# Input projection of a hybrid decoder trunk: twelve of thirteen products in the two-bank, 512-column form

## What is computed

```python
z = x @ w_in[l]                      # 256 x 1024 times 1024 x 6400
z_s5, z_lx, z_ly, z_rw, z_gate = jnp.split(z, IN_SPLITS, axis=-1)
y_s5  = s5_branch(z_s5, ...)         # diagonal complex state space, scan, gelu(...)
y_lru = rglru_branch(z_lx, z_ly, ..) # conv, gates, scan; y = h * gelu(z_ly)
y_rw  = rwkv7_branch(z_rw, ...)      # token shift, low-rank gates, delta-rule state
gates = sigmoid(z_gate)
merged = gates[0]*y_s5 + gates[1]*y_lru + gates[2]*y_rw
```

## Time and profile before

| What | Value |
|---|---|
| Time, median of three runs | 1608.58 us (1608.37 to 1609.64) |
| Profiled execution: span from first to last instruction | 1606.9 us |
| Profiled execution: its own whole time | not given; the span lies 1.7 us under the median |
| PE busy | 1578.1 us, 98% of the span |
| DVE, ACT, POOL busy | 1248.4, 795.6, 223.1 us |
| Mean granted TensorE clock | 0.997 |

### The profile page before, as it was taken

How to read it: one execution, slowest core, us unless ns; L and a number is a source line. 1 busy time by engine, 2 the same in 40 slices (tenths; PEclk the granted TensorE clock), 3 DMA queues, 4 the chain that set the end, 5 groups by cost and what they waited for, 6 DMA issues and landing times. The chain is left out here.

```text
span 1606.9 us, 31358 instructions
## 1 busy us (share of the span) xinstructions
PE 1578.1 (98%) x13277; PEld 1419.2 (88%) x13277; DVE 1248.4 (78%) x1624; ACT 795.6 (50%) x1018; POOL 223.1 (14%) x163
## 2 busy tenths in 40 slices
PE   9999999999999999999999999999999999999997
PEld 8888899999999988888888888999999999888886
DVE  6799789798667858766688998898976778587666
ACT  4655453763454545444455555346533545454443
POOL 2024500000000302001110435000000003010101
PEclk9999999999999999999999999999999999999999
DMA  8766654433536545666676665554345465456663
GB/s 250 215 191 183 183 142 139 134 116 113 178 114 205 177 133 164 192 186 193 207 197 187 190 180 153 159 157 123 106 139 151 128 208 164 143 165 190 189 191 131
DMA packets 380915, 267.74 MB, mean 167 GB/s; under 512 B 21132, under 2 KB 361576, under 8 KB 380776
## 3 DMA queue, kind: packets, MB, share of 16 engines
q1 hardware_dynamic: 377548, 255.16, 53.5%
q10 hardware_dynamic: 3228, 10.58, 2.0%
HBM read 264.66 MB, written 1.05 MB: 165 GB/s over the span
## 5 line engine op out<-in xcount | busy, mean ns | idle before, releaser
L1829 DVE TENSOR_TENSOR ring_lo<-ring_raw,ring_hi 128x1024 fp32r<-128x1024 f32 x461 | 591.9, 1288 | 193.7 <-ACT ring_hi L1410 189.3
L1410 ACT ACTIVATE ring_hi<-ring_raw 128x1024 fp32r<-128x1024 f32 x472 | 497.6, 1057 | 455.3 <-PE bank L765 204.2
L762 PE MATMUL bank<-xT,ring_hi 128*128 128x512 f32 x1344 | 335.5, 391 | 0.0
L762 PEld LDWEIGHTS bank<-xT,ring_hi 128*128 128x128 f32 x1344 | 244.2, 189 | 45.5
L735 PE MATMUL bank<-xT,ring_hi 128*128 128x256 f32 x864 | 252.2, 292 | 4.0 <-DVE region_a L2293 3.6
L736 PE MATMUL bank<-xT,ring_hi 128*128 128x256 f32 x864 | 245.1, 284 | 0.0
L737 PE MATMUL bank<-xT,ring_lo 128*128 128x256 f32 x864 | 244.9, 283 | 0.0
L765 PEld LDWEIGHTS bank<-xT,ring_lo 128*128 128x128 f32 x1344 | 183.3, 190 | 13.3 <-DVE ring_lo L1829 0.3
L765 PE MATMUL bank<-xT,ring_lo 128*128 128x256 f32 x1344 | 187.5, 282 | 0.0
L735 PEld LDWEIGHTS bank<-xT,ring_hi 128*128 128x128 f32 x864 | 166.1, 192 | 10.0 <-DVE region_a L2293 3.9
L736 PEld LDWEIGHTS bank<-xT,ring_hi 128*128 128x128 f32 x864 | 166.2, 192 | 0.6 <-issue 0.5
(11 more groups left out here) (353 smaller groups left out, 2514.7 us busy)
## 6 DMA issues: line engine op xcount, KB each, us to landing
ring_raw<-in_w_in_dram SPq DMA_DIRECT2D x100, 512.0 KB, 4.0
ring_raw<-in_ffn_wg_dram SPq DMA_DIRECT2D x88, 512.0 KB, 4.1
ring_raw<-in_ffn_wu_dram SPq DMA_DIRECT2D x88, 512.0 KB, 4.0
ring_raw<-in_ffn_wd_dram SPq DMA_DIRECT2D x88, 512.0 KB, 3.6
ring_raw<-in_xa_wkv_dram SPq DMA_DIRECT2D x32, 512.0 KB, 3.9
ring_raw<-in_s_glu_w_dram SPq DMA_DIRECT2D x16, 512.0 KB, 3.4
ring_raw<-in_mix_w_out_dram SPq DMA_DIRECT2D x16, 512.0 KB, 4.3
ring_raw<-in_xa_wq_dram SPq DMA_DIRECT2D x16, 512.0 KB, 4.3
```

Of the source, the lines that this page charges most:

```text
L762: mm(both, hi[:, k, :], xT_both[:, :, k, :], start=(k == 0), stop=(k == ND - 1), skip_group_check=True)
L1410: return nc.scalar.activation(o, i, func, **kw)
L1829: st.mark(tt(lo_flat(n), raw_flat(n), hi_flat(i), ALU.subtract), s_lo["dve"])
```

## The change

Chunks N1 to N12 of the projection take the wide form. Each half now has a bank of its own, so a z chunk takes two turns of the rotation. ACT copies each bank whole (both its halves, 128 x 512) to one of four places in `work`, and POOL adds the two halves (128 x 256) into `zu`, `lx`, `ly` or `zrw`. Waits for a z chunk become waits for POOL's sum. The Gelu on `ly` goes out of the copy; it is one ACT operation (128 x 1024) after the Gelus of the S5 output, and DVE waits for it (`s_lyg`) before it uses `ly` at L2339. N0, the gate chunks and everything else stay as they are.

```diff
+def added_later(kind, j):
+    return kind == "z" and j != 0
+def banks_of(kind, j):
+    return 2 if added_later(kind, j) else BANKS_OF.get(kind, 0)
+SUMS = [x for x in PLAN if added_later(*x)]
-ROTA = [(x, b) for x in PLAN for b in range(BANKS_OF.get(x[0], 0))]
+ROTA = [(x, b) for x in PLAN for b in range(banks_of(*x))]
+        halves_z = [view(work, 4096 + 512 * i, 2, T) for i in range(4)]
+        def half_count(kind, j, m):
+            return 2 * SUMS.index((kind, j)) + m + 1
         def released(item, b):
             kind, j = item
+            if added_later(kind, j):
+                return s_half, half_count(kind, j, b)
...
-                elif kind in WIDE:
+                elif kind in WIDE or added_later(kind, j):
...
+                def half_copy(kind, j, m):
+                    n = half_count(kind, j, m)
+                    if n > 4:
+                        act.wait_ge(*at(s_hsum, n - 4))
+                    act.wait_ge(*at(s_piece, INDEX[(kind, j, m)] + 1))
+                    st.mark(f(half_place(kind, j, m), bank(rota(kind, j, m), 2, T), ACT.Copy), s_half)
                 for j in ZORD:
                     hi_to("z", j, ahead=1)
-                    done_chunk(act, "z", j)
-                    func = ACT.Gelu_apprx_tanh if j in (4, 5) else ACT.Copy
-                    st.mark(f(dst[j], bank(rota("z", j), 2, T), func), s_z)
+                    if j == ZORD[0]:
+                        done_chunk(act, "z", j)
+                        st.mark(f(zu[:, 0:2, :], bank(rota("z", j), 2, T), ACT.Copy), s_z)
+                    else:
+                        half_copy("z", j, 0)
+                        half_copy("z", j, 1)
...
+                    if g:
+                        act.wait_ge(*at(s_hsum, half_count("z", ZORD[-1], 1)))
...
+                st.mark(f(ly, ly, ACT.Gelu_apprx_tanh), s_lyg)
...
-                dve.wait_ge(*at(s_z, 9))
+                dve.wait_ge(*at(s_hsum, half_count("z", ZORD[8], 1)))
...
+                dve.wait_ge(*at(s_lyg, 1))
...
+                def half_sum(o, kind, j, m):
+                    pool.wait_ge(*at(s_half, half_count(kind, j, m)))
+                    x = half_place(kind, j, m)
+                    st.mark(tt(o, x[:, 0, :], x[:, 1, :], ALU.add), s_hsum)
+                for j in ZORD[1:]:
+                    for m in range(2):
+                        half_sum(z_to[j][:, m, :], "z", j, m)
```

More of the change, by code:

```diff
@@ L420, in trunk @@
         s_rots = sem("rotation_act", 4)
-        s_z = sem("z_evacuated", 13)
+        s_z = sem("z_first_evacuated", 1)
+        s_lyg = sem("lru_branch_gelu", 1)
         s_k0 = sem("s5_k0_product", 1)
@@ L491, in trunk @@
         s_gact = sem("gates_activated", 12)
+        s_half = sem("halves_copied", 2 * len(SUMS))
+        s_hsum = sem("halves_added", 2 * len(SUMS))
         s_glu = sem("glu_sigmoid", 4)
@@ L514, in sum_count, with half_place @@
             return 4 * (int(kind[1]) * (NF // 2) + j) + (2 if kind[0] == "u" else 0) + m + 1
+        def half_count(kind, j, m):
+            return 2 * SUMS.index((kind, j)) + m + 1
+        def half_place(kind, j, m):
+            return (halves_z)[(half_count(kind, j, m) - 1) % 4]
         def released(item, b):
             kind, j = item
+            if added_later(kind, j):
+                return s_half, half_count(kind, j, b)
             if kind in WIDE:
@@ L532, in released @@
             if kind == "z":
-                return s_z, ZORD.index(j) + 1
+                return s_z, 1
             if kind == "gate":
@@ L983, in s5_in @@
                         if t == 2:
-                            pe.wait_ge(*at(s_z, 2))
+                            pe.wait_ge(*at(s_hsum, half_count("z", ZORD[1], 1)))
                         pe.wait_ge(*at(s_fwd, 2 * t))
@@ L1556, in _ @@
                 prep_evac("bT", (2, 3))
-                dst = {0: zu[:, 0:2, :], 1: zu[:, 2:4, :], 2: lx[:, 0:2, 3:], 3: lx[:, 2:4, 3:],
-                       4: ly[:, 0:2, :], 5: ly[:, 2:4, :]}
-                dst.update({6 + k: zrw[:, 2 * k:2 * k + 2, 1:] for k in range(7)})
                 act.wait_ge(*at(s_bce, 6))
@@ L2278, in _ @@
                 st.then(ins, s_bonr)
-                dve.wait_ge(*at(s_z, 11))
+                dve.wait_ge(*at(s_hsum, half_count("z", ZORD[10], 1)))
                 convolve(0)
@@ L2636, in _ @@
                 st.then(g.memset(lx[:, :, 0:3], 0.0), s_zz)
+                def half_sum(o, kind, j, m):
+                    pool.wait_ge(*at(s_half, half_count(kind, j, m)))
+                    x = half_place(kind, j, m)
+                    st.mark(tt(o, x[:, 0, :], x[:, 1, :], ALU.add), s_hsum)
+                z_to = {1: zu[:, 2:4, :], 2: lx[:, 0:2, 3:], 3: lx[:, 2:4, 3:], 4: ly[:, 0:2, :], 5: ly[:, 2:4, :]}
+                z_to.update({6 + k: zrw[:, 2 * k:2 * k + 2, 1:] for k in range(7)})
+                for j in ZORD[1:]:
+                    for m in range(2):
+                        half_sum(z_to[j][:, m, :], "z", j, m)
                 pool.wait_ge(*at(s_nrm, 1))
```

## The result

The changed kernel takes 1620.73 us, median of five runs (1617.37 to 1622.8), beside 1608.58 us of the kernel before, here also over five runs (1606.87 to 1609.64). The ratio is 1.0072, 95% interval 1.006 to 1.0084. It is slower, by 12.2 us where the forecast had 3.8, and above the top of the range, 1617.0. The profiled executions differ by 12.5 us in span: 1619.4 against 1606.9.

The account below looks back on a forecast made before the run. PE was taken to bound the z stage, DVE close behind. Adds and bank waits start 9b 2.6 us late; after 0.63 saved, the stage ends 1.9 to 2.0 later, +3.8 in two layers: 1612.4 us, range 1606.0 to 1617.0.

Parts of the forecast that it names:

- PE's saving: z stage: a wide half takes 2.79 us instead of 2.88, 0.09 saved per half, 4.3 us if nothing else moves.
- the cover of ACT's work: z stage: ACT's 12 more copies a layer, 7.2 us, fall where ACT waited for PE and cost nothing.
- The bank claim: Halves 7b and 9b wait for S5 output banks DVE releases; without adds the stage ends 0.7 us earlier per layer.
- The price of an add, 0.33 us: DVE chain before the first release: seven of ten POOL adds cost 0.33 us each, 2.3 us together.
- the bound of 4.3: Upper bound for the ten adds up to the first release: 10 x 0.43 = 4.3 us.
- The sign that I named for a wrong forecast: z stage: the forecast is wrong if L1829 stays at 1.22 us beside adds.
- DVE's wait of 0.46 is gone: Between the two releases: DVE, now late, loses its 0.46 us wait; three costly adds there add 1.0 us.
- The remainders are wanted 1.82 us later: Wide z halves want weight remainders 1.82 us later, so DVE lags no further than PE.
- (A): Rival: adds don't touch the DVE chain, only the bank wait is there: 1607.1 us, chance 0.20.
- (B): Rival: PE is never held at 7b and keeps its whole saving: 1604.3 us, chance 0.14.
- (D): Rival: the two-operand product runs no faster than two narrow ones: 1613.7 us, chance 0.16 together with (C).
- (C): Rival: every add costs DVE the dearer 0.43 us: 1617.7 us, chance 0.16 together with (D).

Follow-up runs that it names:

- e3: Changed kernel with POOL's adds replaced by memsets that read nothing and the S5 output's bank released one `s5_half` sooner: 1601.52 us, ratio 0.9962.
- e1: Changed kernel with POOL's 24 adds a layer replaced by memsets of the same targets, which read nothing: 1606.56 us, ratio 0.9988.
- e6: Changed kernel with each POOL add replaced by a copy of one half, reading one operand instead of two: 1614.02 us, one time.
- e2: Changed kernel with the S5 output's bank released one `s5_half` sooner, adds kept: 1614.06 us, ratio 1.0037.
- e4: Changed kernel with the bank released one `s5_half` sooner and N2 to N9's adds timed to run beside DVE's PSUM products: 1606.11 us, ratio 0.999.
- e5: Changed kernel with half 7a's eight 512-column matmuls done twice in each layer: 1620.89 us, ratio 1.0078.
- e7: e4 with DVE making the weight remainder of gate chunk 0's second half before the last token shift: 1606.85 us, ratio 0.9992.
- e8: Kernel before, narrow form, with only 24 POOL adds a layer on spare columns added, results unused: 1618.42 us, one time.
- e9: Changed kernel with half 7a's eight 512-column matmuls done three times in each layer: 1616.81 us, ratio 1.0053.

## Why the prediction was wrong

The direction, the place and both mechanisms were as forecast; the price and the number of costly adds were set too low, and two consequences of PE's stop were left out: the lower clock and the wait that comes back to DVE.

- **PE's saving and the cover of ACT's work**: right. Unhindered, they come to 2.38 us a layer in e3 against 2.50 worked out.
- **The bank claim**: right. In e1, 7b starts at 253.28 as said, and the second release starts at 268.08, 0.17 ahead of 268.25; its end was put 0.29 ahead.
- **The price of an add, 0.33 us**: the first step that failed. It measured 0.50 to 0.55. Counted to the first release, eight of the eleven adds cost and not seven of ten. From the chain's start (217.16) to L2218's (257.65) DVE took 40.49 us, before 36.62 (216.57 to 253.19); with the lost wait of 0.21 that is 4.08, eight by 0.51. I had 2.3. It is inside the bound of 4.3 that I gave, and I took the lower part of it because both prices came from L1829. L1829 was the wrong witness in another way too: in this stretch its mean stayed at 1.22, even where adds came up during it, since the price then fell on the scan, sum or product behind. The sign that I named for a wrong forecast, L1829 at 1.22 beside adds, came true, with the mechanism sound.
- **"DVE's wait of 0.46 is gone"**: failed, and with it the second stretch. I had 15.06 - 0.46 + 1.0 = 15.6 us between the releases; it was 17.45 (257.65 to 275.10): one costly add, 0.54, and a wait of 2.28. PE's lateness comes back to DVE through `s5_in(3)`. I let DVE delay PE and forgot that PE then delays DVE. In e6 the same wait is 2.28 behind a fall of the clock and 0.54 without one, so most of it, 1.7, comes of the lower clock.
- **The granted clock**: not in the prediction at all. PE's stop was followed by 3.3 us at 1.2 GHz, 1.8 us more for half 7b. In e6 such a fall is worth 1.54 us of the stage; if it is worth as much here, it is 3.1 of the 8.3 us by which the forecast fell short.
- **"The remainders are wanted 1.82 us later"**: failed. 5a's second pass stopped 1.37 us for one; in e2, without the claim, four such stops make 3.4 us. A margin of 1.82 us is three adds or so. In the changed kernel the stop at 5a does not add to the end of the stage, since PE waits for the bank behind it anyway.

Added up in the measured times, 9b starts 66.41 us after N0's last matmul (275.64 - 209.23), before 60.07: 6.34 later, of which 3.71 stand at the first release, 2.39 between the releases and 0.24 at 9b itself. The last seven halves and what follows give 0.46 back: 5.88. The forecast had 1.91 (2.3 less 0.39), 0.54 and 0.18, and 0.63 back: of the 3.9 us that it missed per layer, 1.8 lie in the price and the number of the adds up to the first release and 1.85 in the stretch between the releases.

**The rivals.** (A), the bank claim alone, is e1: 1606.56 measured, 1607.1 worked out. (B) has no support: PE was held. (D) falls with e3, where the wide form pays in full. (C), every add at the dearer price and a time of 1617.7, came nearest, with a price of 0.43. The rule of the Trainium skill, "SBUF — State Buffer", section "Who interferes with whom", led to about 1618. The runs agree with its condition for two SBUF inputs on DVE beside a read by POOL. An operation that only writes (e1) costs nothing, and the PSUM products (e4) are not stretched. On the size, the page has the later instruction wait for the whole of the earlier one, and the trace comes close to that if an add is counted from the end of the DVE operation during which it came up: 0.59 and 0.60 us, against 0.55 and 0.53 too long. Two SBUF inputs are not the whole condition in these runs: L2256, a product of one large SBUF operand with a column of parameters, took 0.82 us beside an add and 0.34 without (ns min/median/max):

```profile
L2256 DVE TENSOR_SCALAR work<-region_z,param_columns x8: 341/580/819, 292.6 to 1096.6; 128x256 f32<-128x256 f32 x8
```

## What to carry to other kernels

Before moving an elementwise step to an idle engine, ask what its reads do to the busy engine beside it: here each 128x256 add on POOL with such an operation behind it took half a microsecond from a DVE that had 8 us in 88 to spare. Once a delay makes PE stop, walk the loop right round, since the stopped engine's own products are inputs of the engine that held it, and count the lower clock behind the stop. If the work must go there, time it to run beside operations with a PSUM operand.

## What the runs showed of the hardware that I had not expected

- The length of PE's stop does not decide alone whether the clock falls. It fell after stops of 3.38 us (after, both layers), 1.83 (e5, both layers), 2.53 (e6, layer 0) and 0.58 (e7, layer 1); it did not after the same 2.53 in e6's layer 1, 2.03 in e8 (both layers), 1.67 in e9 (both) 1.11 in e1 (both) and 0.59 in e7's layer 0. A stop of 1.8 us for L2293 (L2331) in a later stage is in every kernel whose waits I read; after it the clock fell in some profiled executions and not in others: in the one of before in layer 1 alone, in e1 and e3 in both layers, in e2 and e9 in neither. What decides it no run here shows. In e6 one fall was worth 1.54 us, so this is likely a part of the spread between runs of one kernel.
- DVE's scans and short sums pay as much beside an add (0.50 to 0.55) as a 1.22 us remainder does (1.76 for one in e9): the price goes by what is left of the add, not by the length of the operation that meets it.
- POOL gets its reads in between DVE operations that follow one another without a gap: in the whole run no add of POOL took over 1.79 us.
